# Fused three-block model on one core: level products of a gated scan split over two engines, a mixer's gate chain and head norms reordered, row biases added on another engine

## What is computed

```
# HGRN2: per head, t >= s, with b the running sum of log f
scores[t, s] = sum_d q[t, d] * k[s, d] * exp(b[t, d] - b[s, d])
# mLSTM: log_d[t, s] = b[t] - b[s] + ig[s];  m[t] = max(b[t] + m_prev, max_s log_d[t, s])
w = (q @ k.T) * exp(log_d - m);  h = w @ v / max(|sum_s w|, exp(-m))
# head norm, both: o * rsqrt(mean(o * o over the head's 128)) * g, then a gate (silu or sigmoid)
# a "row" of the modulation, 1024 wide, in two steps of 512: silu(c) @ w[:, cols] + bias[cols]
```

## Time and profile before

| What | Value |
|---|---|
| Time, median of 3 runs | 2635.36 us (2631.52 to 2641.18) |
| Profiled execution, its own time | 2640.11 us |
| Span of the profiled execution | 2638.3 us |
| TensorE busy | 2353.4 us (89%) |
| VectorE busy | 844.8 us (32%) |
| ScalarE busy | 412.4 us (16%) |
| GpSimd busy | 115.9 us (4%) |
| Granted TensorE clock, mean | 0.931 |

### The profile page before, as it was taken

One profiled execution on the slowest core, in us unless ns is written; L12 is line 12 of the kernel. 1 busy time (PEld: TensorE's weight loads), 2 busy tenths in 40 slices (PEclk: granted clock), 3 DMA queues, 4 the chain that ended last, 5 costly groups with the idle time before them and its releaser, 6 DMA issues. The chain is left out here.

```text
span 2638.3 us, 25405 instructions
## 1 busy us (share of the span) xinstructions
PE 2353.4 (89%) x9952; PEld 1375.0 (52%) x9952; DVE 844.8 (32%) x1734; ACT 412.4 (16%) x889; POOL 115.9 (4%) x81
## 2 busy tenths in 40 slices
PE   6998989888899888888879989898779998989998
PEld 5565633333333333333337678655648763646873
DVE  4554312211122111122236443643366301332301
ACT  1212201111111111111122311112221001221100
POOL 1000000001000010000000000000300000000000
PEclk9977799999999999999989998889889999989999
DMA  8753468999989999999976720464236543323441
GB/s 314 263 217 138 177 245 322 381 412 406 411 305 378 409 397 412 403 409 412 401 300 248 255 80 17 179 247 179 96 128 235 180 152 126 132 86 120 160 143 65
DMA packets 212255, 655.50 MB, mean 248 GB/s; under 512 B 8518, under 2 KB 13182, under 8 KB 195540
## 3 DMA queue, kind: packets, MB, share of 16 engines
q1 hardware_dynamic: 208368, 647.86, 64.8%
q0 software_dynamic: 1712, 3.60, 0.4%
q10 hardware_dynamic: 2004, 1.67, 0.2%
HBM read 652.05 MB, written 1.05 MB: 248 GB/s over the span
## 5 line engine op out<-in xcount | busy, mean ns | idle before, releaser
L1558 PE MATMUL ps<-w,XE 128*64 128x512 f32 x1536 | 363.0, 628 | 66.5 <-DMA w<-in_w_gate_up 63.0
L776 PE MATMUL ps<-HF,w 128*128 128x256 f32 x1408 | 312.7, 385 | 1.8 <-DVE CF L2854 1.8
L776 PEld LDWEIGHTS ps<-HF,w 128*128 128x128 f32 x1408 | 271.8, 194 | 43.6 <-issue 5.7
L1558 PEld LDWEIGHTS ps<-w,XE 128*64 128x64 f32 x1536 | 122.8, 144 | 292.5 <-issue 288.5
L1588 DVE TENSOR_TENSOR T<-ps,BB 128x512 f32<-128x512 f32 x64 | 44.3, 692 | 616.9 <-PE ps L1558 616.9
L611 DVE SCALAR_TENSOR_TENSOR AUX<-w,CS,AUX 128x512 f32<-128x512 f32 (+1 forms) x228 | 169.8, 745 | 8.1
L792 PE MATMUL ps<-w,AF 128*128 128x512 f32 x352 | 151.6, 593 | 1.8 <-DVE AF L2876 1.8
L792 PE MATMUL ps<-w,HT 128*128 128x512 f32 (+1 forms) x352 | 152.8, 589 | 0.3 <-DVE S L1403 0.3
L776 PE MATMUL ps<-HT,w 128*128 128x256 f32 x640 | 146.8, 388 | 5.5 <-DVE dqk L2291 3.7
L1629 PE MATMUL ps<-GR,AT 128*64 128x512 f32 x256 | 120.9, 628 | 31.4 <-DMA AUX<-in_w_down 31.1
L1629 PE MATMUL ps<-w,AT 128*64 128x512 f32 x512 | 121.8, 619 | 18.3 <-DMA w<-in_w_down 17.9
(11 more groups left out here) (568 smaller groups left out, 2666.9 us busy)
## 6 DMA issues: line engine op xcount, KB each, us to landing
w<-in_w_gate_up SPq DMA_DIRECT2D x96, 2048.0 KB, 15.7
w<-in_w_down SPq DMA_DIRECT2D x32, 2048.0 KB, 19.3
w<-in_ada_w SPq DMA_DIRECT2D x24, 2048.0 KB, 7.9
w<-in_ffn_w_in SPq DMA_DIRECT2D x20, 2048.0 KB, 7.9
w<-in_w_in SPq DMA_DIRECT2D x17, 2048.0 KB, 9.3
GR<-in_w_gate_up SPq DMA_DIRECT2D x16, 2048.0 KB, 18.1
AUX<-in_w_gate_up SPq DMA_DIRECT2D x16, 2048.0 KB, 22.8
GR<-in_w_down SPq DMA_DIRECT2D x16, 2048.0 KB, 10.0
```

The source lines that it names most:

```text
L776: ins = e.matmul(out_, w[:, k, c:c + n], HT[:, k, :], start=k == 0, stop=k == kc - 1, skip_group_check=True)
L1558: ins = e.matmul(b[j * n:j * n + n, :], FM.XE[:, side(x), 4 * kh + k, j * n:j * n + n], ring.tile(512, 1024, "gu", ex_, h, kh, x[0])[:, k, ...
```

## The change

- **Row bias.** The matmul of L635 goes. At the end of `ada_acc_dve` a row step gets one more VectorE instruction, which adds the bias row to partition 0 of the sum, after a wait for the row's landing.
- **Levels.** GpSimd multiplies only tile 0 of `KL`; VectorE multiplies tile 1, behind `QL`. GpSimd's and VectorE's waits on the level before go by its tile 0. The stick pieces are dealt out anew: 1, 2 behind level 0; 3, 4 behind 1; 5, 6, 7, 8, 9 behind levels 2, 3, 4, 5, 6.
- **Gate chain of the odd mixer.** The `ccm` transposes move behind the first `oqk` tile, and ScalarE's exp of `CCM` behind its first copies.
- **Head norms.** They run by group of four heads: group 0's straight after its `mo` products, before VectorE and ScalarE turn to group 1. Output gate piece 3 is cut in two: matmuls 0 to 3 stay before the wait for `W`, 4 to 7 go behind group 1's products. The turning goes by group too, and each output gate piece's sigmoid is evicted in its own group.

```diff
--- before.py
+++ after.py
@@ -614,6 +614,12 @@
         dve.leave("w", "ada", n)
         own(e, dve)
         e.tensor_tensor(AC2[:, 2 * i, lo:], AC2[:, 2 * i, lo:], AC2[:, 2 * i + 1, lo:], ADD).then_inc(*dve("ada acc", n))
+        if ADA[n][0] == "row":
+            own(e, dve)
+            e.wait_ge(sems["rows_landed"], ROWS_LANDED[n])
+            j = ADA[n][4]
+            e.tensor_tensor(AC2[0:1, 2 * i, :], AC2[0:1, 2 * i, :], m.ROW[0:1, 512 * j:512 * j + 512], ADD).then_inc(
+                *dve("ada acc", n))
 
     def ada_sum_pe(e, n):
         kind, _, _, _, j, rest, _ = ADA[n]
@@ -630,10 +636,7 @@
                 ins = e.matmul(b[rows, k:k + 1], AC2[:, 2 * i, :].rearrange("q (p k) -> q k p", k=8)[:, k, :], ones[:, 0:1],
                                start=True, stop=True, skip_group_check=True)
         else:
-            e.matmul(b, ones, AC2[:, 2 * i, :], start=True, stop=False, skip_group_check=True)
-            e.wait_ge(sems["rows_landed"], ROWS_LANDED[n])
-            ins = e.matmul(b, ones[0:1, :], m.ROW[0:1, 512 * j:512 * j + 512], start=False, stop=True,
-                           skip_group_check=True)
+            ins = e.matmul(b, ones, AC2[:, 2 * i, :], start=True, stop=True, skip_group_check=True)
         ins.then_inc(*pe("ada summed", n))
 
     def ada_columns_pe(e, n, fs):
@@ -2581,19 +2584,18 @@
             if L:
                 e.wait_ge(*at("decay", i))
                 if i > 1:
-                    e.wait_ge(*at("scores", i - 1, 1))
-                for t in range(2):
-                    own(e, pool)
-                    e.tensor_tensor(heads(KL, 4)[:, :, cols(t)], FE.ka[:, :, cols(t)], FE.lf[:, :, cols(t)], MUL).then_inc(
-                        *pool("KL", i, t))
+                    e.wait_ge(*at("scores", i - 1, 0))
+                own(e, pool)
+                e.tensor_tensor(heads(KL, 4)[:, :, cols(0)], FE.ka[:, :, cols(0)], FE.lf[:, :, cols(0)], MUL).then_inc(
+                    *pool("KL", i, 0))
         ada_step_pool(e, 34)
         end(pool, "pool", "even")
 
 
 
+    STICK_AFTER = ((1, 2), (3, 4), (5,), (6,), (7,), (8,), (9,), ())
+
     def stick_piece_pe(e, s):
-        if s >= 10:
-            return
         name, i = (("eqb", s), ("ekb", s - 4), ("evb", s - 8))[min(s // 4, 2)]
         if i == 0:
             e.wait_ge(*at("w", name))
@@ -2607,8 +2609,6 @@
             pe.leave("w", name)
 
     def stick_piece_act(e, s):
-        if not 0 <= s < 10:
-            return
         name, i = (("eqb", s), ("ekb", s - 4), ("evb", s - 8))[min(s // 4, 2)]
         e.wait_ge(*at(name, i))
         b = bank(name, i)
@@ -2643,8 +2643,8 @@
                     ins = e.matmul(b[:, HC[hd]], kl[:, hd, cols(t)], ql[:, hd, cols(t)], start=True, stop=True,
                                    skip_group_check=True)
                 ins.then_inc(*pe("scores", i, t))
-            stick_piece_pe(e, 1 + 2 * i)
-            stick_piece_pe(e, 2 + 2 * i)
+            for s in STICK_AFTER[i]:
+                stick_piece_pe(e, s)
         e.wait_ge(*at("evb", "out"))
         for hd in range(4):
             b = bank.take(e, "zs", hd)
@@ -2707,11 +2707,8 @@
             if L:
                 e.wait_ge(*at("differences", i))
                 e.activation(flat4(FE.lf), flat4(FE.lf), ACT.Exp).then_inc(*act("decay", i))
-            if i == 0:
-                stick_piece_act(e, 0)
-            else:
-                stick_piece_act(e, 2 * i - 1)
-                stick_piece_act(e, 2 * i)
+            for s in STICK_AFTER[i - 1] if i else (0,):
+                stick_piece_act(e, s)
         e.wait_ge(*at("K1 diff"))
         e.activation(FE.K1[:, :], FE.K1[:, :], ACT.Exp).then_inc(*act())
         e.activation(heads(FE.Q1[:, :], 4), FE.bcu[:, :, 128:256], ACT.Exp).then_inc(*act("K1Q1 exp"))
@@ -2764,7 +2761,7 @@
                 ev = lf.rearrange("p (n l) -> p n l", l=2 * L)
                 bm = v[:, :, L - 1:L].broadcast_to([128, 1024 // (2 * L), L])
                 if i > 1:
-                    e.wait_ge(*at("KL", i - 1, 1))
+                    e.wait_ge(*at("KL", i - 1, 0))
                     own(e, dve)
                 e.tensor_tensor(ev[:, :, 0:L], bm, v[:, :, 0:L], SUB).then_inc(*dve())
                 e.tensor_tensor(ev[:, :, L:2 * L], v[:, :, L:2 * L], bm, SUB).then_inc(*dve("differences", i))
@@ -2772,6 +2769,8 @@
                 if i > 1:
                     e.wait_ge(*at("scores", i - 1, 1))
                 e.tensor_tensor(QL, flat4(FE.qa), lf, MUL).then_inc(*dve("QL", i))
+                e.tensor_tensor(heads(KL, 4)[:, :, cols(1)], FE.ka[:, :, cols(1)], FE.lf[:, :, cols(1)], MUL).then_inc(
+                    *dve("KL", i, 1))
             mask = C(f"H{L}") if L else ident
             for t in range(2):
                 e.wait_ge(*at("scores", i, t))
@@ -2902,21 +2901,35 @@
             e.dma_start(FO.GBI[:, g:g + 1], src[g, :].rearrange("(p o) -> p o", o=1)).then_inc(sems["gate_b_landed"], 16)
         end(pool, "pool", "odd")
 
-    def og_piece_pe(e, s):
+    def og_piece_pe(e, s, ks=range(8)):
         hf, t = s // 2, s % 2
-        if t == 0:
-            e.wait_ge(*at("w", "og", hf))
-        b = bank.take(e, "og", hf, t)
-        tok_pe(e, b, ring.tile(1024, 512, "og", hf), 0, 512, FO.HT, t).then_inc(*pe("og", s))
-        if t:
-            pe.leave("w", "og", hf)
+        w = ring.tile(1024, 512, "og", hf)
+        if ks[0] == 0:
+            if t == 0:
+                e.wait_ge(*at("w", "og", hf))
+            bank.take(e, "og", hf, t, hold=True)
+        ins = tok_pe(e, bank("og", hf, t), w[:, ks[0]:ks[-1] + 1, :], 0, 512, FO.HT, t, ks[0], ks[0] == 0, ks[-1] == 7)
+        if ks[-1] == 7:
+            ins.then_inc(*pe("og", s))
+            bank.drop("og", hf, t)
+            if t:
+                pe.leave("w", "og", hf)
+
+    def odd_heads_pe(e, g):
+
+        for k in range(4 * g, 4 * g + 4, 2):
+            b = bank.take(e, "OTo", k)
+            for t in range(2):
+                e.wait_ge(*at(("hno", g, t), "out"))
+                for j in range(2):
+                    ins = e.transpose(b[:, j * 256 + t * 128:j * 256 + t * 128 + 128], FO.O[:, t, cols(k + j)], ident)
+            ins.then_inc(*pe("OTo", k))
 
     def og_piece_act(e, s):
-        if s >= 0:
-            hf, t = s // 2, s % 2
-            e.wait_ge(*at("og", s))
-            e.activation(FO.OG[:, t, 512 * hf:512 * hf + 512], bank("og", hf, t), ACT.Sigmoid).then_inc(*act("og", "out"))
-            act.leave("bank", "og", hf, t)
+        hf, t = s // 2, s % 2
+        e.wait_ge(*at("og", s))
+        e.activation(FO.OG[:, t, 512 * hf:512 * hf + 512], bank("og", hf, t), ACT.Sigmoid).then_inc(*act("og", "out", s))
+        act.leave("bank", "og", hf, t)
 
     def odd_pe(e):
         features(e, "odd")
@@ -2927,14 +2940,14 @@
             ins = feat_pe(e, b[0:8, 256 * g:256 * g + 256], w, 8 * g, 8, FO.HT)
         ins.then_inc(*pe("ogates"))
         pe.leave("w", "gates")
+        feats_pe(e, ("oqk", 0), ("oqk", 0), ring.tile(1024, 512, "oqk", 0), 4, FO.HT)
         b = bank.take(e, "ccm")
         e.wait_ge(*at("igcm"))
         for t in range(2):
             e.transpose(b[:, 16 * t:16 * t + 8], IG[:, cols(t)], ident[0:8, 0:8])
             ins = e.transpose(b[:, 16 * t + 8:16 * t + 16], NMX[:, cols(t)], ident[0:8, 0:8])
         ins.then_inc(*pe("ccm"))
-        for g in range(2):
-            feats_pe(e, ("oqk", g), ("oqk", g), ring.tile(1024, 512, "oqk", g), 4, FO.HT)
+        feats_pe(e, ("oqk", 1), ("oqk", 1), ring.tile(1024, 512, "oqk", 1), 4, FO.HT)
         for hf in range(2):
             toks_pe(e, ("ov", hf), ("ov", hf), ring.tile(1024, 512, "ov", hf), FO.HT)
         for g in range(2):
@@ -2954,7 +2967,7 @@
                          skip_group_check=True)
                 e.matmul(b[:, 256:384], FO.CO[hp, 4 + hd // 2, 128:256], FO.CO[hp, hd // 2, 128:256], start=True, stop=True,
                          skip_group_check=True).then_inc(*pe("mqk", hd))
-            og_piece_pe(e, 2 * g + 1)
+            og_piece_pe(e, 2 * g + 1, range(4 if g else 8))
             e.wait_ge(*at("W", g))
             if g == 0:
                 e.wait_ge(*at(("ov", 1), "out"))
@@ -2968,8 +2981,9 @@
                             ins = e.matmul(b[:, 129 * j:129 * j + 129], FO.W[:, i + j, c:c + 128], FO.VX[:, k, hd, :],
                                            start=k == 0, stop=k == t, skip_group_check=True)
                     ins.then_inc(*pe("mo", g, t, i))
-        e.wait_ge(*at(("hno", 1), "out"))
-        turn_pe(e, "OTo", lambda t, k: FO.O[:, t, cols(k)], 8)
+        og_piece_pe(e, 3, range(4, 8))
+        for g in range(2):
+            odd_heads_pe(e, g)
         features(e, "OTo")
         out_pe(e, "outo", ((1024, 0),), FO.HT)
         norm_pe(e, m.ffn[1], "ffn1")
@@ -2982,13 +2996,14 @@
         e.activation(BS, BS, ACT.Exp, scale=-1.0).then_inc(*act())
         own(e, act)
         e.activation(BS, BS, ACT.Ln, bias=1.0).then_inc(*act("o softplus"))
```

(40 more changed lines are left out.)

## The result

The changed kernel takes 2591.27 us (median of 4 runs, 2586.49 to 2596.05) against 2633.44 us of the kernel before beside it: ratio 0.9835 [0.9806, 0.9863], 42 us less. The forecast was 2600.0 in a range of 2588 to 2619. The profiled execution took 2586.49 us (span 2584.4, granted clock 0.946; before 2640.11, 2638.3 and 0.931).

A forecast was written before the change was run, and what follows sets the result against it. TensorE, busy 89% of the span, was taken as the bound nearly everywhere. Terms 16.4 + 6 + 9.4 + 5.5 = 37.3 us gave 2602.8 from the profiled 2640.11 and 2598.1 from the median 2635.36; forecast 2600, range 2588 to 2619.

The forecast's parts named there:

- Row bias: Fourteen row steps: each loses the bias matmul on TensorE and VectorE gets an add of 0.70 us; 16.4 us gained.
- Levels: Even mixer: VectorE always wins, GpSimd's tile takes 2.9 us, cycle 8.1 us; 6 us gained, bounds -2 and +9.
- Gate chain: Odd mixer: TensorE's gap between gates and projections goes, with its fall of the clock; 9.4 us gained, bounds 7.5 and 10.
- Head norms: Odd mixer: output matmuls start sooner after the last product; 5.5 us gained, bounds 1 and 7.
- the first stage's 6.1 us are kept: Row steps before the experts: their gain lasts, since the expert stage's loads are issued as that stage's slots come free.
- the price of the ten later steps: Row steps from n = 16 on: 1.05 us each at full clock, 2.00 at half, nothing at n = 40, 1.0 at n = 41.
- At n = 41: Row step where TensorE waits for VectorE's L616: 1.77 us go, 0.75 us of add come; 1.0 us gained.
- the landing is hidden: VectorE's wait for the bias row, 1.8 to 8.6 us after issue, does not delay TensorE, even at n = 34.
- The rival in which VectorE becomes the bound there: Around the row steps, VectorE's add and the landing wait leave rows 3 us instead of 16; 2613 us, chance 0.12.
- the other side of the lock: Levels: GpSimd goes after QL, VectorE's tile waits for it; cycle 7.5 us, 8.6 us gained, 2597 us; chance 0.20.
- the cover of 1.3 us before `W`: Odd mixer, group 1: W ready at 2342.0, TensorE there at 2343.3; each microsecond beyond the cover is lost.
- The slower case: TensorE stays at 1.2 GHz through levels, short products and output projection; 41 us slower, 2676 us; chance 0.02.

The follow-up runs named there:

- e2: Only the level edits (tile 1 of KL on VectorE, pieces dealt out anew) on the kernel before: 2634.11 us, ratio 1.0000.
- e3: Only the gate-chain edits of the odd mixer on the kernel before: 2631.18 us, ratio 0.9983.
- e4: Only the head-norm edits (norms by group, output gate piece 3 cut in two) on the kernel before: 2629.67 us, ratio 0.9971.
- e6: Only the second tile of KL moved to VectorE, pieces where they were, on the kernel before: 2641.27 us, ratio 1.0005.
- e7: Only the pieces dealt out anew, both tiles of KL still on GpSimd, on the kernel before: 2634.31 us, ratio 0.9994.
- e9: The changed kernel with the one-row bias matmuls put back: 2618.22 us, ratio 0.9936 against the kernel before.
- e10: The changed kernel with TensorE's sum of step 41 behind the first tile of the feed-forward's second half: 2590.23 us, ratio 0.9826 against the kernel before.
- e12: The changed kernel with the edits of e8, e10 and e11 together: 2584.82 us, ratio 0.9798 against the kernel before.
- e8: The changed kernel with all four level products on VectorE, none on GpSimd: 2590.17 us, ratio 0.9826 against the kernel before.
- e5: The changed kernel itself, the same file, run again: 2596.53 us, ratio 0.9838 against the kernel before.
- e11: The changed kernel with tile 0's head norm ahead of output gate piece 3's sigmoid: 2604.84 us, ratio 0.9873 against the kernel before.

## Why the prediction was right, point by point

**Row bias: near in size by luck, two terms wrong.** Forecast 16.4 us; the runs give 18 alone and 22 to 26 in the changed kernel, the stretches of the table with row steps 20.7.

The first term that was wrong is "the first stage's 6.1 us are kept". Seven traces have the bias product (the kernel before, e2, e3, e4, e6, e7, e9) and seven don't. On average TensorE comes to the router at 264.1 us with it and at 259.7 without, 4.4 earlier. The expert stage then takes 1096.7 us with it (1094.8 to 1099.7) and 1101.6 without (1098.8 to 1104.0), and its end is at 1360.8 and 1361.3: nothing is left of the first stage's gain. On each of the three chips of the experiments the expert stage is the longer one without the product. The two traces of the table hide this, since the kernel before's has the longest expert stage of its seven. In that stage TensorE waits 105 to 118 us for weight loads in all 14 traces, some 50 times; that the loads don't move with its earlier start is the likely cause, not shown.

The second is the price of the ten later steps: forecast 10.3 us, and their four stretches give 17.0 in the table and 19 by the averages of the same traces (without e10 and e12 in ffn0, where e10's edit works). The price 1.05 at the full clock counts the bias product alone. The chain before, around the bias products of n = 31, 35 and 41:

```profile
1787.66 0.86 PE ps L633 x2
1788.52 1.05 PE ps L635 x2
1789.57 13.93 PE ps L792 x32
...
1978.85 15.48 PE ps L776 x64
...
2068.69 78.81 PE ps L776 x352
```

And after, the same places:

```profile
1769.66 0.86 PE ps L639 x2
1770.52 13.73 PE ps L795 x32
...
1943.57 14.45 PE ps L779 x64
...
2032.27 76.65 PE ps L779 x352
```

A step with its product, from sum to sum, is 15.84 us before (0.86 + 1.05 + 13.93) and 14.59 after (0.86 + 13.73): the product behind the bias matmul also gets 0.2 us shorter, so a step is worth 1.25. Behind n = 35 the sum and 64 records took 2.05 + 2.00 + 15.48 = 19.53 us and take 2.04 + 14.45 = 16.49: 3.0 us and not 2.00, since the clock comes back sooner. The 7 us from the start of the sum, before and after (the columns of the earlier trace rows):

```profile
1974.80:1981.80 7.00, 7.00 (x11) 3.46 (x12) 6.64 (x10) 0.00 (x0) 0.49 (x1) 0.50 0.11 18
```

```profile
1941.50:1948.50 7.00, 6.97 (x23) 5.26 (x24) 6.66 (x10) 0.00 (x0) 0.49 (x1) 0.77 0.19 50
```

From the start of the sum it takes 7.0 to 10.1 us until the projection's matmuls come at the distance of the full clock in the seven traces with the bias product, and 2.7 to 3.4 us in the seven without; at n = 41 it is 8.1 to 9.7 against 3.1 to 3.4. Why the half clock lasts longer with the bias product is not shown. At n = 41 the forecast was 1.0, and up to the end of its sum that is right (89.9 us from the stage's start before, 88.9 after); but the 352 records behind it take 2.16 us less, and at the stage's end eight transposes take 1.08 instead of 1.95. The add was 0.68 us on one partition, forecast 0.70, and the landing is hidden, as forecast. The rival in which VectorE becomes the bound there fell: beyond the 0.7 us counted at n = 41, what it costs TensorE is the 0.6 us at n = 17.

**Levels: the size right, the mechanism the rival's.** I had VectorE win the port always: GpSimd's tile 2.9 us, cycle 8.1. It is the other side of the lock. The timeline after, one level:

```profile
1825.57 1.23 DVE L2771 TENSOR_TENSOR XE<-eqa,elf 128x1024 f32<-128x1024 f32 x1 [1.12 <-ACT elf L2709]
1825.62 2.31 POOL L2589 TENSOR_TENSOR XE<-eka,elf 128x512 f32<-128x512 f32 x1 [6.96 <-ACT elf L2709]
1826.72 1.76 DVE L2772 TENSOR_TENSOR XE<-eka,elf 128x512 f32<-128x512 f32 x1
```

GpSimd's tile takes 2.31 us, as before, and VectorE's second product 1.76 instead of the 0.68 that it takes in e8 with GpSimd away. Each waits its turn: GpSimd for `QL`, then VectorE's tile 1 for GpSimd. That fits the Trainium skill, "SBUF — State Buffer", section "Who interferes with whom", by which the two exclude each other for a whole instruction in the order of issue; e8 shows its other half, no wait without GpSimd. The cycles, from the starts of scores:

```profile
1829.19 1.80 PE ps L2643 x16
...
1836.75 2.04 PE ps L2643 x16
...
1844.56 2.68 PE ps L2643 x16
...
1853.00 2.02 PE ps L2643 x16
...
1861.89 1.78 PE ps L2643 x16
```

7.6 and 7.8 us; 8.4 behind the scores of 2.68, part of them at the half clock; then 8.9 with a long piece. The scores of levels 6 and 7 came down from 3.77 to 1.78 and 1.80, as forecast. The stage gives 5.5 to 8.6 us by the clock's luck; the forecast's 6 us and the rival's 8.6 are both in it, so the size could not have told them apart. Alone it adds nothing to the total that the runs can tell (e2), in the whole (e9) it can't be told apart. Where e2's 5.4 us went is open: its trace shows 2.9 us more in ffn0, but e4, which leaves the levels alone, has the same 255.5 us there.

**Gate chain: right.** No gap of TensorE is left behind the gates (chain after, against the earlier trace rows):

```profile
2189.09 1.08 PE ps L886 x8
...
2191.93 23.73 PE ps L779 x96
2215.66 0.15 PE ps L2947
...
2216.00 14.01 PE ps L779 x64
```

From the gates to the v projection it is 37.9 us, before 46.2: 8.3 less, and 9.5 less in e3 (36.7), forecast 9.4. The 1.2 us between the two are in the gates and the first weight tile, 23.73 us here and 22.53 in e3, more of it at the half clock. The total of e3 alone gave half of it, with 9 just inside the interval.

**Head norms: right, one step off.** Forecast 5.5. The chain after, against the earlier trace rows:

```profile
2292.21 1.96 DVE WO L3088 x4
...
2294.22 2.95 PE ps L2981 x24
2297.16 3.45 PE ps L795 x8
...
2301.77 1.28 ACT L1074
...
2307.66 0.70 PE ps L2925 x2
...
2310.22 29.29 PE ps L795 x64
```

From the last `mo` product's end (2297.16) to the output product it is 13.06 us, forecast 12 to 13. The stretch from the first broadcast is 7.6 us shorter (60.4 to 52.8), and the output product pays 1.6 back, 29.29 for 27.72, since it starts behind idle time at the lower clock: 6.0. The step that was off is the cover of 1.3 us before `W`. `W` was ready 36.8 us after the first broadcast, forecast 36.9; TensorE was early, since output gate piece 2 took 7.06 us where it had taken 8.76 before, part of it at the lower clock. So TensorE waited the 0.2 us of the wait list.

**The sum.** Forecast 37.3; by stage the terms are 21 + 6 to 9 + 8 + 6, or 41 to 44, and the runs say 39 (e5) to 42. Single stages move with the execution (the one before the even projections, with no part of the change, took 78.3 us here and 81.2 in e5, whose code is the same). The term that was mis-sized is the row bias, twice: 6.1 us of it in front of the expert stage were not kept, and the other ten steps brought 17 to 19 us instead of 10.3, since a matmul taken out of a slow stretch is worth more than its own time. That the two errors nearly cancel is luck. The slower case, the clock staying at its lower level through the levels, fell: 0.93 and 0.88 there, 0.84 before.

## What to carry to other kernels

Price an instruction taken off a saturated TensorE by the distance between the groups around it, not by its own piece of the chain: here 1.25 us for 1.05, and 3.0 for 2.00 in a slow stretch. Then follow the gain through the next stage that waits for its loads: here 4.4 us at the router were gone at the end of the experts. Before work is split between VectorE and GpSimd, see whether both read two operands from SBUF; if so the second engine may add only its queue: here the faster one alone was better by 4 to 7 us of the stage. On ScalarE count the table loads of a new order, and ask whose bank the delayed eviction holds: e11 lost 4.5 us of its stage so.

## What the runs showed of the hardware

- VectorE's product of 128x512 beside a running GpSimd product of the same size takes 1.76 us, alone 0.68; GpSimd's takes 2.31 beside VectorE's of 1.23, alone 1.28 (e7).
- An add on one partition with 512 columns takes 0.68 us on VectorE, a subtraction on 128 partitions with as many columns 0.69: between these two the partitions cost nothing.
- The same code in the second block took 80.0 to 88.3 us from one execution to another, with the granted clock in its latter half at 0.87 and 0.62. Runs of one kernel scatter by 10 to 23 us (the kernel before, 2623.04 to 2645.68 us in 16 runs), so a part of 5 us needs a stage's landmarks beside many runs, and neither is enough alone.
- Switching ScalarE between root, exp and sigmoid costs 1.28 us each time, and nothing more: the chain goes on 0.01 to 0.02 us behind the load (e11).
- With a matmul of one row of ones (1x512) between the sum and the projection, TensorE stayed at 1.2 GHz for 7.0 to 10.1 us after it started again at n = 35, without it for 2.7 to 3.4 us, in seven traces each.
